# Expert blocks of 32 tokens on four column groups, gate and up in one pass, and wide VectorE instructions for the gathered rows

## What is computed

```python
aff = sigmoid(h @ router_w)                  # 16 experts in 4 groups
e_idx = top 2 experts of the best group      # per token: 1024 assignments
for each block of rows of one expert e:
    xb = h[row_token]
    out = (silu(xb @ w_gate[e]) * (xb @ w_up[e])) @ w_down[e]
y = sum over a token's two experts of weight * out
x = x + mx[5] * y
```

## Time and profile before

| | us |
|---|---|
| median of 3 runs (1397.36 to 1401.35) | 1397.66 |
| profiled execution, span | 1399.6 |
| PE busy in it | 1237.5 |
| expert stage of layer 0, first gate matmul to end of last down product | 306.9 |
| the same of layer 1 | 283.2 |

### The profile page before, as it was taken

How to read it: one execution, slowest core, us unless ns; L and a number is a source line. 1 busy time by engine, 2 the same in 40 slices (tenths; PEclk the granted TensorE clock), 3 DMA queues, 4 the chain that set the end, 5 groups by cost and what they waited for, 6 DMA issues and landing times. The chain is left out here.

```text
span 1399.6 us, 18544 instructions
## 1 busy us (share of the span) xinstructions
PE 1237.5 (88%) x6619; PEld 642.5 (46%) x6620; DVE 434.6 (31%) x951; ACT 349.9 (25%) x670; POOL 334.8 (24%) x491
## 2 busy tenths in 40 slices
PE   4899969888898399999999769999985799999992
PEld 1744425444444255555555334444442455555550
DVE  1222775763223422222222241111226122222223
ACT  2311115564402132222222220000011322222220
POOL 1000059940000123333333220000010333333331
PEclk9999986887799699999999989999997899999996
DMA  9918771110014299879899680401335798989995
GB/s 336 352 61 297 262 282 61 61 61 0 1 60 164 105 392 389 319 289 347 319 394 395 251 333 0 163 18 57 124 105 195 272 388 324 366 324 391 396 367 194
DMA packets 138558, 322.47 MB, mean 230 GB/s; under 512 B 7452, under 2 KB 8520, under 8 KB 138514
## 3 DMA queue, kind: packets, MB, share of 16 engines
q1 hardware_dynamic: 127250, 294.44, 57.1%
q0 software_dynamic: 8640, 23.09, 4.5%
q10 hardware_dynamic: 2624, 4.33, 0.8%
HBM read 307.15 MB, written 19.92 MB: 234 GB/s over the span
## 5 line engine op out<-in xcount | busy, mean ns | idle before, releaser
L1604 PE MATMUL bank<-ring,apad 128*64 128x256 f32 x2176 | 251.7, 385 | 6.3 <-ACT apad L742 3.2
L1604 PEld LDWEIGHTS bank<-ring,apad 128*64 128x64 f32 x2176 | 156.3, 139 | 99.7 <-issue 29.0
L1682 PE MATMUL bank<-hT_cat,ring 128*128 128x512 f32 x384 | 165.0, 592 | 1.0 <-ACT hT_cat L612 1.0
L1620 PE MATMUL scores<-ring,apad 128*64 128x512 f32 x544 | 124.2, 598 | 1.9 <-DVE apad L1156 1.9
L742 ACT ACTIVATE apad<-scores,modcol,mod_a 128x64 f32<-128x64 f32 x208 | 67.2, 403 | 210.3 <-PE scores L1589 210.3
L1682 PEld LDWEIGHTS bank<-hT_cat,ring 128*128 128x128 f32 x384 | 72.9, 190 | 92.5 <-issue 91.4
L1274 POOL COPY cur_idx<-row_i 128x1 int32 (+1 forms) x56 | 10.1, 181 | 383.2 <-ACT apad L751 307.2
L1238 POOL TENSOR_SCALAR stats<-stats 128x1 f32<-128x1 f32 x18 | 8.5, 471 | 343.9 <-ACT mid L602 332.8
L1162 DVE SCALAR_TENSOR_TENSOR prob<-scores,slot_w,qT 128x512 f32<-128x512 f32 x50 | 37.6, 751 | 132.8 <-PE scores L1620 132.8
L925 DVE SCALAR_TENSOR_TENSOR mid<-apad,taps,mid 128x512 f32<-128x512 f32 x90 | 75.6, 880 | 0.6
L1152 DVE TENSOR_TENSOR apad<-apad,bank 128x256 f32<-128x256 f32 x50 | 21.1, 421 | 175.6 <-PE bank L1604 175.6
(11 more groups left out here) (248 smaller groups left out, 1557.9 us busy)
## 6 DMA issues: line engine op xcount, KB each, us to landing
ring<-in_w_mod SPq DMA_DIRECT2D x24, 2048.0 KB, 17.3
ring<-in_moe_w_gate SPq DMA_DIRECT2D x22, 2048.0 KB, 11.6
ring<-in_moe_w_up SPq DMA_DIRECT2D x22, 2048.0 KB, 11.8
ring<-in_moe_w_down SPq DMA_DIRECT2D x22, 2048.0 KB, 11.2
mid<-in_moe_w_gate SPq DMA_DIRECT2D x10, 2048.0 KB, 11.3
hT_cat<-in_moe_w_up SPq DMA_DIRECT2D x10, 2048.0 KB, 12.0
big<-in_moe_w_down SPq DMA_DIRECT2D x10, 2048.0 KB, 11.4
ring<-in_od_w_in SPq DMA_DIRECT2D x6, 2048.0 KB, 19.2
```

The source lines that it names most:

```text
L1604: mm = T.matmul(ps[h * BLK:(h + 1) * BLK, 0:256], hgT[:, k, :], w[:, k, h * 256:(h + 1) * 256], start=(k == 0), stop=(k == KD - 1))
L1620: mm = T.matmul(y_ps[h * BLK:(h + 1) * BLK, :], actT[:, k % 2, (k // 2) * BLK:(k // 2 + 1) * BLK], wd[:, k, h * 512:(h + 1) * 512], start= ...
L1682: mm = T.matmul(ps[:, :], w[n][:, k, i * P:(i + 1) * P], hT_cat[:, k, :], start=(k == 0), stop=(k == KD - 1))
```

## The change

A block becomes 32 tokens. A partition now holds a quarter of a token's row, 256 elements, so that 32 tokens again fill 128 partitions; every gather and scatter still has 128 rows, of 1 KB in place of 2 KB. Gate and up are one product: for each of the 8 chunks there are four matmuls, one for each column group of 32, and each streams 256 columns, 128 of gate and 128 of up, which lie in neighbouring slots of `ring` (now of nine slots, with `mid`, `hT_cat` and `big` as views into it). They end in one bank, `gu_ps`. The transposes of the product of the block before stand in the middle, after four chunks, and are one transpose where they were two. Those of the gathered rows are two where they were four. Down is 4 chunks of four matmuls of 256 columns where it was 4 of two of 512. The modulation leaves ACT: DVE does it in two instructions of 256 elements with scale and shift broadcast along the tokens, with a semaphore between them. It does so ahead of the product of the same iteration. A block's gate and up wait for the product of the block before.

Not shown: constants and tile widths that follow from BLK, and `xhat_d`, `y_d` and their views, with 256 in place of 512 elements a row.

```diff
-BLK = 64
+BLK = 32
+NQ = P // BLK
...
-        ring = sb("ring", [P, RING, KD, 512])
+        ring = sb("ring", [P, RING + 3, KD, 512])
+        mid = ring[:, RING].rearrange("p k n -> p (k n)")
+        hT_cat = ring[:, RING + 1]
+        big = ring[:, RING + 2].rearrange("p k n -> p (k n)")
...
-                used = (gate_done[l], up_done[l], down_done[l])
+                used = (gu_done[l], gu_done[l], down_done[l])
...
                 with act.Fori(0, total) as b:
-                    act.wait_ge(gate_done[l], b + 1)
+                    act.wait_ge(gu_done[l], b + 1)
                     act.wait_ge(act_ready[l], b + 1)
-                    act.activation(silu_g, gate_ps[:, 0:256], ACT.Silu).then_inc(silu_ready[l], 1)
+                    act.activation(silu_g, gu_ps[:, 0:P], ACT.Silu).then_inc(silu_ready[l], 1)
 
                     act.wait_ge(hg_turned[l], b + 2)
-                    act.wait_ge(up_done[l], b + 1)
-                    turn_in()
                     move_on(b + 3)
...
+                def turn_in(b_plus_1):
+
+                    dve.wait_ge(hg_turned[l], b_plus_1)
+                    V.tensor_tensor(chunks(hg_scaled_sb), hg_ps[:, 0:2 * P].rearrange("p (i q s) -> p q i s", i=2, q=NQ), scale,
+                                    ALU.mult).then_inc(hg_scaled[l], 1)
+                    dve.wait_ge(hg_scaled[l], b_plus_1)
+                    V.tensor_tensor(chunks(hgT), chunks(hg_scaled_sb), shift, ALU.add).then_inc(hgT_ready[l], 1)
...
                 with dve.Fori(1, total) as b:
 
                     product_turned(b)
+                    dve.wait_ge(gu_done[l], b + 1)
+                    turn_in(b + 2)
                     product(b)
-                    dve.wait_ge(hg_turned[l], b + 2)
-                    turn_in()
                     result(b - 1)
...
-                G.tensor_tensor(y_out, y_blk, const("ones")[:, 0:1].to_broadcast([P, 512]), ALU.mult).then_inc(y_moved[l], 1)
+                G.tensor_tensor(y_out, y_blk, const("ones")[:, 0:1].to_broadcast([P, 256]), ALU.mult).then_inc(y_moved[l], 1)
...
-                    T.matmul(ps[h * 64:(h + 1) * 64, :], const("sel_x")[:, 0:64], modrow[:, :], start=True, stop=False)
-                    mm = T.matmul(ps[h * 64:(h + 1) * 64, :], bias_row.to_broadcast([P, 64]), b_rows[:, :], start=False, stop=True)
+                    for q in (2 * h, 2 * h + 1):
+                        rows, cols = slice(q * BLK, (q + 1) * BLK), slice(q % 2 * 256, q % 2 * 256 + 256)
+                        T.matmul(ps[rows, 0:256], const("sel_x")[:, 0:BLK], modrow[:, cols], start=True, stop=False)
+                        mm = T.matmul(ps[rows, 0:256], bias_row.to_broadcast([P, BLK]), b_rows[:, cols], start=False, stop=True)
...
-                    for j in range(4):
-                        mm = T.transpose((hg_dve_ps, hg_act_ps)[j // 2][:, j % 2 * P:(j % 2 + 1) * P], hg_next[:, j * P:(j + 1) * P], ident)
+                    for i in range(2):
+                        mm = T.transpose(hg_ps[:, i * P:(i + 1) * P], hg_next[:, i * P:(i + 1) * P], ident)
...
+                def gate_up(par, chunks):
+
+                    slot = EXPERT_SETS[l][par][0]
+                    for k in chunks:
+                        for q in range(NQ):
+                            mm = T.matmul(gu_ps[q * BLK:(q + 1) * BLK, 0:2 * P].rearrange("p (w n) -> p w n", w=2), hgT[:, k, :],
+                                          ring[:, slot:slot + 2, k, q * P:(q + 1) * P], start=(k == 0), stop=(k == KD - 1))
+                    return mm
...
-                    for k in range(4):
-                        for h in range(2):
-                            mm = T.matmul(y_ps[h * BLK:(h + 1) * BLK, :], actT[:, k % 2, (k // 2) * BLK:(k // 2 + 1) * BLK],
-                                          wd[:, k, h * 512:(h + 1) * 512], start=(k == 0), stop=(k == 3))
+                    for k in range(NQ):
+                        for n in range(NQ):
+                            mm = T.matmul(y_ps[n * BLK:(n + 1) * BLK, :], actT[:, k, :], wd[:, k, n * 256:(n + 1) * 256],
+                                          start=(k == 0), stop=(k == NQ - 1))
...
-                    pe.wait_ge(hgT_dve[l], b * 4 + 4)
-                    pe.wait_ge(hgT_act[l], b * 4 + 4)
-                    half_columns(gate_ps, landed(i, par, 0), gate_done[l])
+                    pe.wait_ge(hgT_ready[l], b + 1)
+                    pe.wait_ge(act_ready[l], b + 1)
+                    landed(i, par, 0)
+                    landed(i, par, 1)
+                    gate_up(par, range(KD // 2))
                     turn_product(b)
-                    half_columns(up_ps, landed(i, par, 1), up_done[l])
+                    gate_up(par, range(KD // 2, KD)).then_inc(gu_done[l], 1)
                     turn(b + 2)
                     down(b, i_before, par_before)
```

More of the change, by code:

```diff
@@ L83, in build_consts @@
     add("slot_of_col", np.tile(p % BLK, (P, 1)))
-    add("half", p // BLK)
-    add("out_offset", p // BLK + 2 * NIDX)
+    add("quarter", p // BLK)
+    add("out_offset", p // BLK + NQ * NIDX)
     add("full_blocks", np.tile(np.arange(SEQ // BLK) * BLK - (np.arange(SEQ // BLK) == 0), (P, 1)))
@@ L1597, in landed @@
                     pe.wait_ge(unit_in[slot], i * 16 + (moe_base[l][slot] + 1) * 16)
-                    return expert_view(slot, "wd" if k == 2 else "wg")
-                def half_columns(ps, w, done):
-                    for k in range(KD):
-                        for h in range(2):
-                            mm = T.matmul(ps[h * BLK:(h + 1) * BLK, 0:256], hgT[:, k, :], w[:, k, h * 256:(h + 1) * 256],
-                                          start=(k == 0), stop=(k == KD - 1))
-                    mm.then_inc(done, 1)
+                def gate_up(par, chunks):
[5 more added lines that the diff above has]
+                    return mm
@@ L1608, in turn_product @@
                 def turn_product(b_plus_1):
                     pe.wait_ge(act_ready[l], b_plus_1 + 1)
-                    for j in range(2):
-                        mm = T.transpose(at_ps[:, j * P:(j + 1) * P], act_sb[:, j * P:(j + 1) * P], ident)
-                    mm.then_inc(act_turned[l], 1)
+                    T.transpose(at_ps[:, 0:P], act_sb, ident).then_inc(act_turned[l], 1)
                 def down(b_plus_1, i, par):
-                    wd = landed(i, par, 2)
+                    landed(i, par, 2)
@@ L1642, in later_blocks @@
                             block_of(b, i, par, i, par)
-                pe.wait_ge(hgT_dve[l], 4)
-                pe.wait_ge(hgT_act[l], 4)
-                half_columns(gate_ps, landed(0, 0, 0), gate_done[l])
-                half_columns(up_ps, landed(0, 0, 1), up_done[l])
+                pe.wait_ge(hgT_ready[l], 1)
+                landed(0, 0, 0)
+                landed(0, 0, 1)
+                gate_up(0, range(KD)).then_inc(gu_done[l], 1)
                 turn(2)
```

89 lines of the change are left out of this document (37 added, 52 removed).

## The result

The changed kernel takes 1417.68 us (median of 4 runs, 1412.72 to 1422.13) against 1397.61 us of the kernel before on the same chip: a ratio of 1.0139, 95% interval 1.0112 to 1.0166. It is slower by 20 us, where 1390 was forecast. Medians here and in the table further down take in every execution, ratios only the fast ones, which matters for one of e2 (3961.5 us) and one of e4 (1517.5 us at a granted clock of 0.785).

What follows compares the result with a forecast made beforehand. The prediction took PE to set the pace before the change and two single-buffered round trips after it. Expert stages -9.2 us, routing tables +3.6, entry and exit -2.5: -8 us from 1397.66, so 1390 us, range 1361 to 1418.

Steps and rivals of the forecast that it cites:

- rival of longer round trips: Expert stages: gather and scatter share a queue, 7.7 us a block or more, kernel slower, 1418 us at 8.1; chance 0.28.
- p: Expert stages: time of one block under weight traffic, set by the round trips, forecast as 7.4 us.
- PE's block: Expert block on PE: gate and up 3.6, transposes 0.25 and 0.37, down 1.75, together 6.0 us.
- third rival: Expert matmuls on PE: column groups don't run as computed, loads exposed, 9.1 us a block, 1551 us; chance 0.03.
- Two single-buffered round trips: Expert stages: gather loop 7.2 us and scatter loop 7.3 set the pace, no longer hidden by the block.
- The fourth expert's start: Start of a layer: its up weights land 36.6 us after the first gate matmul, nothing gained until then.
- Half the bytes: Gather's landing: 128 KB less a gather takes 0.5 us off the median of 6.2, giving 5.7.
- DVE's eight narrow operations ... Cost nothing: Modulation in the expert block: two wide DVE instructions, about 0.95 us, hidden while PE transposes and does down (2.1 us).
- the prediction's own formula: Both expert stages together: 936.2 - 2520/p - 2p, giving 580.9 us against 590.1, so -9.2 us.
- under which 28 blocks run; the others take 6.0: Expert stages: 210 us of weight traffic a layer slows 28 blocks, the rest take 6.0 us each.
- Entry and exit of the stage ... -2.5: Ends of each expert stage: shorter last result, y_out and first gather save 1.2 us a layer, 2.5 in all.
- faster: Whole kernel's sign: faster beyond the 4 us from no change, chance 0.48; same 0.17, slower 0.35.

Runs made afterwards that it cites:

- e2: Changed kernel with two buffers for results on their way out, the gather keeping its one buffer: 1416.34 us, ratio 1.0107 to the kernel before.
- e4: Changed kernel, single buffers, with the gather's index copy made ahead of the wait for the move: 1407.14 us, ratio 1.0050 to the kernel before.
- e10: Changed kernel with every scatter issued with an unused block's indices, so that it writes no row: 1397.36 us, one run.
- e1: Changed kernel with two buffers for gathered rows, the scatter keeping its one buffer: 1403.84 us, ratio 1.0022 to the kernel before.
- e11: Kernel before the change, with gathers of half a row (128 KB less a gather): 1402.32 us, one run.
- e9: Changed kernel with the scaled rows between DVE's two wide instructions in a free PSUM bank instead of SBUF: 1407.98 us, ratio 1.0065 to the kernel before.
- e7: Changed kernel with the modulation as before, eight narrow instructions on DVE and ACT instead of two wide ones: 1412.25 us, ratio 1.0081 to the kernel before.
- e6: Changed kernel, single buffers, with PE's block numbers loaded once inside the block instead of three times between blocks: 1414.40 us, ratio 1.0088 to the kernel before.
- e3: Changed kernel with two buffers for both gathered rows and results: 1382.85 us, ratio 0.9864 to the kernel before.
- e5: Changed kernel with both buffers doubled and PE's block numbers loaded once inside the block: 1364.77 us, ratio 0.9720 to the kernel before.

## Why the prediction was wrong

**The chip's answer was the rival's.** The rival of longer round trips gave 1418 for p = 8.1, 1417.68 was measured. Its mechanism, the scatter in flight in the same queue, was not it: e10 takes the scatters' rows away and the median landing stays within 0.06 us.

**Right.** 38 and 42 blocks. PE's block: 3.6, 0.25, 0.37 and 1.75 us, 6.08 measured for 6.0. All four column groups side by side: no row shows the exposed loads of the third rival. Two single-buffered round trips set the pace (e1 to e4), though the gather's is the longer one (e1, e2), where the prediction had 7.2 us for it and 7.3 for the scatter's. 1.12 us from move to gather (1.13 predicted). The fourth expert's start after 36.3 and 37.2 us (36.6). Half the bytes are worth 0.4 to 0.5 us of landing (e11, 0.5 predicted). What the profile was to show came: ACT waits for the landing in most blocks, PE idles before the transposes, and waits 6.8 and 5.5 us for the fourth expert.

**Wrong: the size of p, by two terms.** "I take 0.5, so 5.7 ... p = 7.4" should have been 7.6. Under load the move follows its gather after 6.06 us in the mean, plus 0.42 and 1.13. The first reason is a cost that I put at nothing: "DVE's eight narrow operations ... Cost nothing". I priced them on PE's path only, and there they do hide. But the wide add delays POOL's gather, which is on the loop: 0.15 us in the instruction, and 12 us of stage when it goes (e9). The prediction weighed a rule of the Trainium skill on PE (TensorE: Matmul & The Clock Gate, section on packing small matmuls), which the trace contradicts, and not the one on SBUF under e9, which counted. The second reason is that the median of a loop isn't its mean: medians of 5.8 go with means of 5.92 to 5.94 even in e7 and e9. By the prediction's own formula p = 7.6 instead of 7.4 is worth 8.6 us, with the weight traffic as long as it had assumed.

**Wrong: "under which 28 blocks run; the others take 6.0".** 62 moves waited at full length (30 and 32), where 57 were forecast (28 a layer). The traffic is spread over more time than 210 us a layer: SP's slots are held by large experts for a while (no weights are issued between 542.8 and 560.4, and none between 626.4 and 643.8), the last issues for an expert come at 741.9 and 1351.5, and in layer 0 the next layer's dense weights follow at once, from 743.5. At p = 7.6 the assumed traffic would hold 55.3 blocks, so these are 6.7 more, at 7.6 less 6.0 us each: 10.7 us. And at a change of expert PE pays 0.6 to 1.9 us, which was in no term at all; 11.6 us of queued work had covered it before, as a block of 6.1 us does not. It costs 30 us of PE's idle time and, beside late gathers, 4.6 us of stage (e6).

8.6 + 10.7 = 19.3 us, which is nearly all of the 20.1 by which the stages (601.0) missed the forecast (580.9). These two are worked out by the formula, not measured. The wide add (12.1 of stage, e9) is a part of them. The loads (4.6, e6) and the low clock behind the fourth expert's wait (2.4 + 1.9, which was in no term either) would come on top and carry the sum 8 us too far, so something overlaps or runs faster than the formula has it, and no run splits that. That the first two close the sum by themselves is partly luck.

**Wrong: "Entry and exit of the stage ... -2.5".** From the end of layer 0's stage to layer 1's first gate matmul it is 308.1 us, before 301.2 (by the windows of the earlier trace rows). The tables are in it with 1.9 us (1.8 predicted a layer), and 1.7 us come back between the tables and the first gate matmul. Some 5 us are the exit, and another 1.5, between the read-back and the routing, are not traced. At the exit the rings run behind PE when it stops, and the last results wait for a gather of an unused block.

```profile
772.81 1.06 POOL L1270 DMA_INDIRECT kv_buf<-xhat_d,cur_idx  x1 [0.50 <-issue]
773.89 0.63 POOL L1275 TENSOR_TENSOR kv_buf<-prob,cst 128x256 f32<-128x256 f32 x1
774.73 0.48 DVE L1155 SCALAR_TENSOR_TENSOR prob<-scores,slot_w,qT 128x256 f32<-128x256 f32 x1 [5.28 <-POOL kv_buf L1275]
778.02 0.60 POOL L1275 TENSOR_TENSOR kv_buf<-prob,cst 128x256 f32<-128x256 f32 x1 [1.52 <-DMA y_d<-kv_buf,cur_idx]
782.04 3.77 SPq L530 DMA_DIRECT2D ring<-y_d  x8
```

The last down product ends at 771.5; the results are read back from 782.0, 10.5 us later (before 5.5, in e3 6.1). One of DVE's last results waits 5.28 us for POOL. e3 brings the stretch back to 303.0 us.

**The range** held the time, at its edge. I gave "faster" 0.48 with a margin of 0.1 us in p: the forecast said p = 7.4, faster ended at 7.49, slower began at 7.69. A forecast that hangs on a tenth of a microsecond in a term bounded from 3.4 to 7.9 had no ground for the sign.

## What to carry to other kernels

Smaller blocks shorten the engine's part of a loop and leave its latencies as they are: before halving a block, list every single-buffered round trip and every per-block or per-group scalar load that the long block hid, then double the buffers and move the loads in the same step (e3, e5: from +1.4% to -2.8%). Two loops of nearly the same length must be opened together; one alone shows two fifths of the gain (e1), or hardly any (e2). And cost an instruction on the engines that share something with it, not only on its own path: an operation with both inputs in SBUF on VectorE that starts just ahead of GpSimd's DMA issue delays it, and with one input in PSUM it didn't (e9).

## What the runs showed of the hardware

- A wide DVE add with both inputs in SBUF that starts 0.14 us before POOL's indirect DMA instruction lengthens it from 1.06 to 1.21 us; with one input in PSUM it doesn't (e9). At distances from 0.07 to 0.24 us the gather's instruction ended 1.35 us after the add's start. The two are released by the same event, so they met in 35 blocks at the same distance.
- A load of a number from SBUF into a register of PE between two blocks is not hidden by queued matmuls when a block is 6.1 us long: three of them cost 0.6 us, and 1.9 us after an inner loop. One load amid the matmuls costs next to nothing (e5).
- From issue to move, which waits for the landing, a gather of 128 x 1 KB took 2.8 to 3.6 us beside paused weight traffic and 6.06 us in the mean beside full traffic. 128 KB less in a gather took 0.4 us off the median landing (6.2 to 5.8, e11).
- While PE stood still for 6.84 us in the midst of a stage the granted clock fell from 1.00 to 0.50, it stayed there for the first 5 us of work, and 32 matmuls of 256 columns took 3.64 us instead of 1.93.
- 5120 weight loads of 32 columns ran inside the gate-and-up matmuls of four column groups, with every group on the same rows: 164.5 us of loads beside 322.2 us of matmuls in e3, with blocks at 6.08 us.
